# A hybrid encoder block with 32 experts: last expert's results summed by TensorE, row numbers made on GpSimd, logits with operands exchanged, norm stage and first unit in another order

## The reference

```python
u2 = rms_norm(h, norm_ffn_g)
logits = u2 @ router_w + router_b                  # 512 x 32
top_val, top_idx = lax.top_k(logits, 4)
gates = jax.nn.softmax(top_val)
# for each token n, choice k and expert e = top_idx[n, k]:
#   glu, lin = split(u2[n] @ w1[e] + b1[e])        # 1024 -> 2 x 1024
#   act = min(glu,7) * sigmoid(1.702*min(glu,7)) * (clip(lin,-7,7) + 1)
#   y[n, k] = act @ w2[e] + b2[e]                  # 1024 -> 1024
h = h + sum_k gates[n, k] * y[n, k]
out = rms_norm(h, final_norm_g)[:, 16:]
```

## Time and profile before

| | us |
|---|---|
| timed runs, median (lowest, highest) | 1636.83 (1635.07, 1637.48) |
| profiled execution, whole | 1649.01 |
| its span, first to last instruction | 1647.2 |
| PE busy | 1585.5 (96%) |
| DVE, POOL, ACT busy | 650.5, 427.5, 392.4 |
| first dense product starts | 22.21 |
| last dense add on DVE starts | 536.18 |
| first expert starts on PE | 565.95 |
| last product of the last expert ends | 1617.60 |

### The profile page before, as it was taken

The page is one execution under the profiler, slowest core; times in us unless marked ns, Lnnn a source line. Parts: engine busy times, 40 slices in busy tenths (PEclk is TensorE's granted clock), DMA queues, the critical chain, the costliest instruction groups (busy, mean ns, idle before and its releaser), DMA issues.

```text
span 1647.2 us, 38590 instructions
## 1 busy us (share of the span) xinstructions
PE 1585.5 (96%) x16312; PEld 1113.2 (68%) x16312; DVE 650.5 (39%) x1233; ACT 392.4 (24%) x599; POOL 427.5 (26%) x465
## 2 busy tenths in 40 slices
PE   6999999998999889999999999999999999999992
PEld 6998988876889756655556566666666666556551
DVE  3799897025151523322332232224222322232238
ACT  4333134255122512211221111111112111221121
POOL 6334334371433611111111112111211121112114
PEclk9999999999999899999999999999999999999996
DMA  7563243320275289999999999999999999999995
GB/s 212 176 193 118 78 143 89 101 81 22 93 291 195 83 330 412 412 397 410 407 405 392 407 405 399 397 406 406 392 401 408 404 393 407 409 405 392 406 394 208
DMA packets 135055, 497.35 MB, mean 302 GB/s; under 512 B 17417, under 2 KB 76977, under 8 KB 85252
## 3 DMA queue, kind: packets, MB, share of 16 engines
q1 hardware_dynamic: 114452, 467.08, 72.2%
q0 software_dynamic: 8880, 16.54, 3.2%
q10 hardware_dynamic: 11680, 13.12, 2.4%
HBM read 478.41 MB, written 27.36 MB: 307 GB/s over the span
## 4 chain that ended last, share of the span: by engine, by line
PE 91%; ACT 2%; DVE 2%; POOL 2%; DMA 1%; issue 1%; SPq 0%; POOLq 0%; ACTq 0%; DVEq 0%
PE banks L1413 40%; PE banks L1019 25%; PE banks L1462 21%; PE banks L1399 2%; DVE mix_lo L1744 1%; DMA stage<-in_w_in_dram 1%; PE banks L1363 1%; ACT w_hi L733 0%; DMA y_last<-y_rows 0%; ACT banks L924 0%; POOL small L574 0%; PE banks L1433 0%; ACT conv L887 0%; DVE gates L1742 0%; POOL w_lo L596 0%
## 5 line engine op out<-in xcount | busy, mean ns | idle before, releaser
L1413 PE MATMUL banks<-w_ring,xT 128*32 128x512 f32 x6144 | 687.9, 592 | 0.7 <-issue 0.7
L1413 PEld LDWEIGHTS banks<-w_ring,xT 128*32 128x32 f32 x6144 | 359.4, 110 | 287.9 <-issue 122.0
L1462 PE MATMUL banks<-w_ring,actT 128*32 128x256 f32 x6144 | 370.7, 381 | 4.8 <-issue 4.8
L1462 PEld LDWEIGHTS banks<-w_ring,actT 128*32 128x32 f32 x6144 | 249.3, 110 | 110.3 <-issue 18.6
L1843 DVE TENSOR_TENSOR hid<-banks,bias 128x512 f32<-128x512 f32 x96 | 63.9, 666 | 477.2 <-PE banks L1413 475.7
L596 POOL TENSOR_TENSOR w_lo<-stage,w_hi 128x2048 fp32r<-128x2048 f32 x38 | 175.2, 4610 | 268.0 <-ACT w_hi L733 268.0
L1019 PE MATMUL banks<-u_hi,w_hi 128*128 128x264 f32 (+1 forms) x544 | 181.3, 333 | 4.5 <-POOL w_lo L587 4.2
L1019 PE MATMUL banks<-u_hi,w_lo 128*128 128x264 f32 (+1 forms) x544 | 179.9, 331 | 0.0
L1019 PE MATMUL banks<-u_lo,w_hi 128*128 128x264 f32 (+1 forms) x544 | 179.6, 330 | 0.0
L990 ACT ACTIVATE bias<-banks 128x512 f32<-128x512 f32 x32 | 19.1, 597 | 572.5 <-PE banks L1433 572.5
L667 POOL COPY token_now<-token_of 96x1 int32 (+1 forms) x33 | 6.5, 198 | 565.1 <-PE banks L1399 560.6
(11 more groups left out here) (269 smaller groups left out, 1626.4 us busy)
## 6 DMA issues: line engine op xcount, KB each, us to landing
w_ring<-in_expert_w_dram SPq DMA_DIRECT2D x384, 1024.0 KB, 11.5
stage<-in_w_in_dram SPq DMA_DIRECT2D x20, 1024.0 KB, 5.3
y_rows<-empty_row ACTq DMA_DIRECT2D x8, 1280.0 KB, 5.4
stage<-in_w_in_dram SPq DMA_DIRECT2D x16, 512.0 KB, 5.2
y_in<-y_rows SPq DMA_DIRECT2D x4, 2048.0 KB, 12.8
stage<-in_conv_pw_w_dram SPq DMA_DIRECT2D x4, 1024.0 KB, 5.4
stage<-in_mlstm_out_w_dram SPq DMA_DIRECT2D x4, 1024.0 KB, 5.2
stage<-in_w_out_dram SPq DMA_DIRECT2D x4, 1024.0 KB, 5.2
```

The costliest lines, as they stand in the source:

```text
L1413: last = nc.tensor.matmul(banks[32 * g:32 * (g + 1), t].rearrange("p (c j) -> p c j", j=64), xT[:, k, 32 * t:32 * (t + 1)], units, start=k ...
L1462: last = nc.tensor.matmul(banks[32 * g:32 * (g + 1), 3 + t, 0:GRP], actT[:, t, k], w2_ring[k // 2][:, k % 2, GRP * g:GRP * (g + 1)], start ...
```

## The change

Five edits, in one kernel.

**First unit.** PE runs it as three passes of 16 products: hi·hi, then lo tokens, then lo weights, each pass with its own wait. The transposes' banks are renumbered (`PART_BANK`), ACT copies five parts instead of four ahead of the first weights, and DVE makes the meta tokens' low part ahead of the last scaling.

**Norm stage.** DVE norms tile i-1 behind the add of tile i; ACT squares all four tiles before it copies `u2T`; POOL scales three tiles before it makes constants, and only those that the router needs before the fourth.

**Logits.** The router's columns become the stationary operand and 128 tokens the moving one, two rounds of four column groups. ACT copies the four partial sums (`part`), and one product with four stacked unit matrices (`stack4`) adds and turns them back.

**Row numbers.** The multiplication of `row_of` moves to POOL, which alone waits for the twelve loads. The shifts and additions go.

**End.** The last expert is taken out of the loop on PE and POOL, and its results aren't stored. Before it, DVE makes `selT`, gate values at (slot, token), and five diagonal matrices of gates. Behind it, PE multiplies `selT` with `y_out`, a row group of 32 slots and a bank for each column group, and adds five of the sixteen gated blocks by diagonal products. DVE sums the other eleven and adds the banks (`add_products`). Tiles 3 and 2 are scaled by ACT and multiplied by POOL, tiles 1 and 0 by DVE as before. The rows for emptying in DRAM are a fifth fewer.

```diff
+TILE_ORDER = (3, 2, 1, 0)
+SUMS = ((3, 0), (3, 1), (3, 2), (3, 3), (2, 0), (2, 1), (2, 2), (2, 3), (1, 0), (1, 1), (0, 0))
+DIAGONALS = ((1, 2), (1, 3), (0, 1), (0, 2), (0, 3))
+SCALED_BY_POOL = (3, 2)
...
-            sp.wait_ge(y_stored, passes * (16 * TG * NE))
-            last_rows = y_dram[Y_ROWS:Y_ROWS + SEQ * CG].rearrange("(i p r) n -> i p (r n)", i=TT, p=P)
-            for i in range(TT):
-                sp.dma_start(y_last[:, i], last_rows[i]).then_inc(y_loaded[TT], 16)
-            for i in range(TT):
-
-                sp.wait_ge(out_made, i + 1)
+            for m, i in enumerate(TILE_ORDER):
+
+                if i in SCALED_BY_POOL:
+                    sp.wait_ge(out_made_pool, m + 1)
+                else:
+                    sp.wait_ge(out_made, m + 1 - len(SCALED_BY_POOL))
                 sp.dma_start(out[0, P * i:P * (i + 1), :], h_res[:, i]).then_inc(stored, 16)
...
-            ffn_norm(0)
-            ffn_norm(1)
+            for i in range(TT - 1):
+                ffn_norm(i)
 
             pool.wait_ge(mm_done, pair_tick(WO_PAIR + 1, 8))
             nc.gpsimd.memset(no_code, NONE).then_inc(moe_consts, 1)
             nc.gpsimd.iota(code, [[TOPK * P, TT], [1, TOPK]], base=0, channel_multiplier=TOPK)
             nc.gpsimd.iota(expert_id, [[1, NE]], base=0, channel_multiplier=0, allow_small_or_imprecise_dtypes=True)
+            nc.gpsimd.memset(all_ones, 1.0)
+            nc.gpsimd.memset(zeros, 0.0)
+            nc.gpsimd.iota(slot_no, [[1, SLOTS]], base=0, channel_multiplier=0, allow_small_or_imprecise_dtypes=True)
+            chain(nc.gpsimd.memset(earlier, 1.0))
+
+            nc.gpsimd.affine_select(out=earlier, in_=earlier, compare_op=ALU.is_gt, fill=0.0, base=0,
+                                    pattern=[[1, P]], channel_multiplier=-1).then_inc(moe_consts, 1)
+            ffn_norm(TT - 1)
...
-            pool.wait_ge(tables_made, 2)
+            pool.wait_ge(rows_in, 16 * CG * TG)
+            chain(nc.gpsimd.tensor_scalar(row_of, row_of, float(CG), group_of, ALU.mult, ALU.add))
...
+            before = CHUNKS + TT
+            for m, i in enumerate(TILE_ORDER[:2]):
+                pool.wait_ge(squared, before + m + 1)
                 rstd(P, f_square[:, i:i + 1], f_rstd[:, i:i + 1], D, rstd_made)
+            for m, i in enumerate(SCALED_BY_POOL):
+                pool.wait_ge(squared, before + 2 + m + 1)
+                if m == 0:
+                    pool.wait_ge(row_bc_in, 48)
+                nc.gpsimd.tensor_tensor(h_res[:, i], h_res[:, i], last_g, ALU.mult).then_inc(out_made_pool, 1)
+            for m, i in enumerate(TILE_ORDER[2:]):
+                pool.wait_ge(squared, before + 4 + m + 1)
+                rstd(P, f_square[:, i:i + 1], f_rstd[:, i:i + 1], D, rstd_made)
...
-                if j == 4:
+                if j == EARLY:
                     split_hi(0, 0)
...
-                if i:
-                    u2T_part(act, i - 1)
-            u2T_part(act, TT - 1)
+
+            def logit_part(i):
+
+                act.wait_ge(logits_mm, 2 * i + 1)
+                nc.scalar.activation(part[:, i % 2], banks[:, 6 + i % 2, 0:P], ACT.Copy).then_inc(u2T_made, 1)
+
+            u2T_part(act, 0)
+            for i in range(TT):
+                if i + 1 < TT:
+                    u2T_part(act, i + 1)
+                logit_part(i)
 
 
             act.wait_ge(bias_in, 16 * 2 * PARTS)
...
+            for m in range(2):
+                last_square(m)
+            for m, i in enumerate(SCALED_BY_POOL):
+                act.wait_ge(rstd_made, CHUNKS + TT + m + 1)
+                nc.scalar.activation(h_res[:, i], h_res[:, i], ACT.Copy, scale=f_rstd[:, i:i + 1]).then_inc(squared, 1)
+            for m in range(2, TT):
+                last_square(m)
...
 
-            pe.wait_ge(u_lo_made, 2 * TT + 1)
+            def first_terms(n):
+
+                for c in range(2):
+                    for k in range(KT):
+                        hi, lo = weights(0, k, c)
+                        last = nc.tensor.matmul(banks[:, c, 0:HALF], lo if n == 2 else hi, (u_lo if n == 1 else u_hi)[:, k, halves[0]],
+                                                start=n == 0 and k == 0, stop=n == 2 and k == KT - 1)
+                if n == 2:
+                    last.then_inc(mm_done, 1)
+
+            def first_unit():
+
+                pe.wait_ge(u_lo_made, 3)
+                pe.wait_ge(u_hi_made, EARLY)
+                pe.wait_ge(w_hi_made[0], 1)
+                first_terms(0)
+                pe.wait_ge(u_lo_made, EARLY)
+                first_terms(1)
+                wait_weights(0, 0)
+                first_terms(2)
...
+
+                    pe.wait_ge(mask_made, i - 1)
+                for r in range(KT // CG):
+                    for g in range(CG):
+                        k = CG * r + g
+                        last = nc.tensor.matmul(banks[32 * g:32 * (g + 1), 6 + i % 2, 0:P], w_router[:, k], u2T[:, i % 2, k],
+                                                start=r == 0, stop=r == KT // CG - 1, tile_position=(0, 32 * g))
+                last.then_inc(logits_mm, 1)
+
             row_transposes(0)
+            pe.wait_ge(wo_out, TT + 2)
+            row_transposes(1)
             for i in range(TT):
-                if i + 1 < TT:
-                    row_transposes(i + 1)
-                pe.wait_ge(u2T_made, 2 * (i + 1))
-                if i >= 2:
-
-                    pe.wait_ge(mask_made, i - 1)
-                for k in range(KT):
-                    last = nc.tensor.matmul(banks[:, 6 + i % 2, 0:NE], u2T[:, i % 2, k], w_router[:, k], start=k == 0, stop=k == KT - 1)
-                last.then_inc(logits_mm, 1)
+                logit_parts(i)
+                if i + 2 < TT:
+                    row_transposes(i + 2)
+                pe.wait_ge(u2T_made, part_copied(i))
+                nc.tensor.matmul(banks[:, 6 + i % 2, P:P + NE], part[:, i % 2], stack4, start=True, stop=True).then_inc(logits_mm, 1)
...
+                pe.wait_ge(last_set, q + 2)
+                pe.wait_ge(y_made, n * TG + (TG + 1))
+                pe.wait_ge(xT_made, n * 2 + 4)
+                for m, i in enumerate(TILE_ORDER):
+                    first_bank = 0 if m % 2 else 4
+                    mine = [d for d in DIAGONALS if d[0] == i]
+                    if m >= 2:
+                        pe.wait_ge(summed, q * TT + (TT + m - 1))
+                    for t in range(TG):
+                        for g in range(CG):
+                            last = nc.tensor.matmul(banks[:, first_bank + g, 0:GRP], selT[32 * g:32 * (g + 1), t, i], y_out[32 * g:32 * (g + 1), t],
+                                                    start=t == 0, stop=t == TG - 1 and not mine, tile_position=(32 * g, 0))
+                    if mine:
+                        pe.wait_ge(y_loaded[i], q * 16 + 16)
+                    for d in mine:
+                        for g in range(CG):
+                            last = nc.tensor.matmul(banks[:, first_bank + g, 0:GRP], diag[:, DIAGONALS.index(d)],
+                                                    y_in[i][:, d[1], GRP * g:GRP * (g + 1)], start=False, stop=d == mine[-1])
+                    last.then_inc(last_mm, 1)
...
-
-
-            dve.wait_ge(g_in, 32)
-            for i in range(TT):
-                dve.wait_ge(rstd_made, CHUNKS + i + 1)
-                nc.vector.scalar_tensor_tensor(out=u2[:, i], in0=h_res[:, i], scalar=h_rstd[:, i:i + 1], in1=gf_bc,
-                                               op0=ALU.mult, op1=ALU.mult).then_inc(u2_made, 1)
+                    if j and i:
+                        normed_rows(i - 1)
+            normed_rows(TT - 1)
...
+                    for t in range(TG):
+                        own(nc.vector.tensor_tensor(sel_in[:, t], slot_row[:, 32 * t:32 * (t + 1)].unsqueeze(1).to_broadcast(shape),
+                                                    last_rep[:, 0].unsqueeze(2).to_broadcast(shape), ALU.is_equal))
+                    for t in range(TG):
+                        own(nc.vector.tensor_tensor(sel_in[:, t], sel_in[:, t], last_rep[:, 1].unsqueeze(2).to_broadcast(shape), ALU.mult))
+                    nc.vector.tensor_scalar(slot_row, slot_row, float(SLOTS), None, ALU.add)
+                    for d, (i, k) in enumerate(DIAGONALS):
+                        nc.vector.tensor_scalar(diag[:, d], ident, gate_now[:, i, k:k + 1], None, ALU.mult)
+                    nc.vector.transpose(selT.rearrange("p t i c -> p (t i c)"), sel_in.rearrange("p t c s -> p (t c s)")).then_inc(last_set, 1)
...
+                def add_products(m):
+
+                    i, first_bank = TILE_ORDER[m], 0 if m % 2 else 4
+                    dve.wait_ge(last_mm, q * LAST_MMS + (2 + m))
+                    dve.wait_ge(sum_step, q * STEPS_OF_SUM + (3 + SEL_STEPS + max(c for c, (j, _) in enumerate(SUMS) if j == i)))
+                    rows = h_res[:, i].rearrange("p (g n) -> p g n", g=CG)
```

(1 more changed line is left out.)

214 lines of the change are left out of this document (141 added, 73 removed).

## The result

| | before | changed |
|---|---|---|
| timed runs, median (lowest to highest) | 1637.15 (1635.07 to 1637.69) | 1626.72 (1622.37 to 1627.39) |
| profiled execution, span | 1647.2 | 1620.6 |

The ratio is 0.9924, with a 95% interval of 0.9909 to 0.9939. That is a gain of 10.4 us by the medians, and of 12.4 by the ratio, where 23.0 were forecast; 1626.7 lies above the 1614 of the forecast and above its range of 1611 to 1624. The profiles overstate the gain (26.6 us of span), for a reason that turned out to be the centre of the case. All medians and ratios in this document are of fast runs; two of the twelve runs of `half_before_again`, further on, took 3313 and 9277 us and are left out.

What follows compares the result with a forecast made beforehand. PE was taken to bound the kernel through 32 equal expert steps. Gains of 6.0 + 13.0 + 4.0 = 23.0 us, subtracted from the timed median of 1636.83, gave 1613.8, or 1614, with a range of 1611 to 1624.

Steps and rivals of the forecast that it cites:

- the experts are 32 equal steps set by PE: Expert loop: PE alone sets each step of 32.66 us; no piece of the chain is a transfer.
- nothing later would eat the first unit's gain: Behind the first unit: 448 us of chains hang on PE's own progress, so the 6.0 us carries through.
- What bounds the kernel: Whole kernel: PE bounds the experts, with the weight stream near at 402 GB/s; gains lie before, around and after them.
- Edit 1: First unit: regrouped passes remove PE's pause and end it at 24.0 instead of 30.06; 6.0 us gained.
- Edits 2 and 3: Norm, logits and row numbers: expert 1 begins at 593.1 instead of 606.1; 13.0 us gained, bounds 10 and 14.5.
- Edit 4: Kernel end, last expert's results added on PE: 4.0 us gained; bounds 5.5 gained to 8.4 lost.
- rival A: Kernel end: products on different row groups don't overlap, 8.4 us lost there, 1626 in all; chance 0.10.
- the drag that was named: Kernel end: POOL's scale steps held by DVE adds, 1.16 us against 0.19; could cost 3 of the 4 us.
- The sum: Whole kernel: 6.0 + 13.0 + 4.0 = 23.0 us, subtracted unchanged from the timed median of 1636.83.
- The 12.2 us between profile and timed runs: Kernel before: profiled execution 1649.01 against timed median 1636.83; the prediction couldn't place the difference.
- Rival B: Expert 1: the early start is lost waiting 5 us for weights, since refills move less than PE; 1619, chance 0.09.
- Rival C: Expert loop: the stream bounds every expert; at 385 GB/s a step is 34.0, 43 us lost, 1657; chance 0.04.

Runs made afterwards that it cites:

- half_before_again: Kernel before, loading only half the columns of each weight piece from expert 1 on (wrong weights, same instructions); 1636.89 us, ratio 0.9991.
- changed, A: The changed kernel in the first comparison, beside the kernel before at 1637.15 us; 1626.72 us, ratio 0.9924.
- changed, D: The changed kernel run once more, beside the kernel before at 1648.50 us; 1628.68 us, ratio 0.9895.
- before_e1: Kernel before with only the first unit's passes regrouped; 1637.92 us, ratio 0.9988.
- rows_on_dve_third: Changed kernel with the row-number multiplication back on DVE, which waits for the twelve row loads; 1623.35 us, ratio 0.9912 (as rows_on_dve 1634.79 us, 0.9916).
- vecs_first: Changed kernel with SyncE's twelve small loads moved between the two halves of the first weights; 1620.54 us, ratio 0.9888.
- long-step set: Runs whose profiles show 32.5 to 32.7 us an expert; the kernel before took 1648.5 us there.
- short-step: Runs whose profiles show 32.24 us an expert; the kernel before took 1637 to 1638.6 us there.
- before_e12: Kernel before with the first unit's passes, norm stage and logits changed; 1642.86 us, ratio 0.9968, and again 1632.71 us, ratio 0.9967.
- C and E: Two sets of runs, each beside the kernel before, which took 1648.45 us in the first and 1638.43 us in the second.
- set D: Set of runs beside the kernel before at 1648.50 us; the changed kernel took 1628.68 us there, ratio 0.9895.
- early3: Changed kernel with expert 1's first three weight pieces refilled ahead of the wait for the scatters and the table loads; 1618.39 us, ratio 0.9872.

## Why the prediction was wrong

| landmark, profiled | before | changed, A | changed, D | `before_e1` | `rows_on_dve_third` |
|---|---|---|---|---|---|
| last dense add | 536.18 | 534.00 | 532.25 | 534.41 | 532.73 |
| expert 0 starts | 565.95 | 558.26 | 557.95 | 568.36 | 557.29 |
| first second product | 592.20 | 579.21 | 578.90 | 592.22 | 582.99 |
| from it to the last one's end | 1025.40 | 1015.98 | 1022.86 | 1011.87 | 1013.99 |
| from there to the end | 29.6 | 25.4 | 25.1 | 33.4 | 25.0 |

The main step that failed is "the experts are 32 equal steps set by PE", carried from the profile of before to the timed runs. There the weight stream is a bound as well, and it took about 7.7 of the 23.0 us. The second is that nothing later would eat the first unit's gain; a wait and half a clock behind it took 3.8 of its 6.0.

**What bounds the kernel** was right for the profiled execution and wrong for the timed ones. At 32.64 us a step the stream wins back lead, at 32.24 it loses some, as the landing times above show. (13.1 MB at the 408 GB/s of the changed kernel are 32.1 us, but 408 was read at PE's own pace, so it doesn't decide it.) The 13 us that PE moved ahead at expert 1 were the lead the stream had lived on. The median landing of 11 us in the earlier trace rows hid a fall from 13.7 to 10.2, so the sign was in the trace of before: 3.5 us won back over the run is little, and the 0.4 us by which a step must have been shorter in the timed runs is more than the 0.15 a step that was won back.

**Edit 1** (6.0 forecast). The unit itself was right: no pause, done at 24.5. "Nothing later eats this" is the second step that failed. A load landing at 26.16 lay 4 us under the old end of the unit, and no chain of before could show it, since PE came later. With the half clock behind it 2.2 were left, and `before_e1` measures 2.0. (From the old end of the unit to the last dense add it is 506 us, where the prediction speaks of 448; nothing hangs on it.) `vecs_first` brings 3.7 at the last dense add.

**Edits 2 and 3** (13.0). Right between the profiles, 13.4: DVE no longer waits for the row loads, there is no hole and no slow pass. Expert 0 came at 24.3 us (24 forecast), expert 1 at 56.5 (57). The scatters moved 6.8 us instead of 3.8, and PE's first-row products ran at the faster rate. The timed runs of single edits show less of it: 5.4 for edits 1 and 2 together, and 4.6 in a long-step set or nothing in a short-step one for the multiplication on POOL; a part of the 8.6 to 9.0 of the next edit, whose runs hold the six shifts, belongs here.

**Edit 4** (4.0). It was undersized: 4.2 between the first two profiles, 4.8 and 5.8 between those of `before_e12` and `rows_on_dve` in C and E, and 8.6 to 9.0 in their timed runs together with the six shifts. Selection products took 1.4 us a tile (2.0 taken), so rival A is out. POOL's first two scale steps took 1.10 and 1.62 beside DVE's sums, the drag that was named, off the path. The old end varies: it is 33.4 in `before_e1`, where DVE waited 3.03 us for the last results; why they came late isn't shown.

**The sum.** "Since the holes named are waits between engines and not recording, I subtract the same 23.0" is where the first failure entered the number, and it cost most. The 12.2 us between profile and timed runs were the other sign that a step was shorter in the timed runs, and 12.2/31 = 0.39 would have given it: 32.25 us a step.

**Rival B** was the mechanism, at a chance of 0.09 and a price of 5 us. It was put aside by a median landing of 11 us and a least of 6.6, which say how far a stream keeps up with a step of 32.64. Its price was 7.7 us by the ratios, not paid once at expert 1: of 4.6 us of waits in the profiled execution 1.2 fall in the second step, most of the rest after the 23rd. So 23.0 less 3.8 (edit 1) less 7.7 gives 11.5, between the 10.4 of the medians and the 12.4 of the ratio. Rival C had the right cause with a bandwidth of 385 GB/s, which wasn't seen. In set D the bare sum holds, 23.0 - 3.8 = 19.2 against 17.3 to 19.8, but partly by luck: an end worth more than forecast stands in it for row numbers that were worth less.

Shown by experiment: that the stream takes a part of the gain, some 7.7 us (half the bytes, the refills earlier, and no wait for a piece in set D), that the small loads caused the wait and the half clock at the start, the part of the row numbers, and the two lengths of a step. Not shown: what the wait at the start costs at the end of the run in a short-step set, what makes the steps of a set long or short, why landing times rise behind 1400 us in the short-step sets, and the timed runs' 4 us above the profiled one, which I take for more of the same waits.

## What to carry to other kernels

When two resources are as near to each other as here (a step of 32.64 lets the stream recover, one of 32.24 does not), treat them as one bound. Before you sum gains on one, look whether the other wins or loses lead from step to step. Landing times by stretch of the run tell it; their median over the whole run doesn't. When a profiled execution and the timed runs of the same kernel differ by more than the runs scatter, divide the difference by the steps of the loop first; the profile may show another balance than the one that is timed. And behind a wait that is removed look for the transfers that land under it: their landing times are in the trace even where nobody waits for them.

## What the runs showed of the hardware

TensorE goes through the same weight loads in two ways that stay the same for a whole set of runs: 82 us of 200 with loads in flight in `before_e1`, 137 in the changed kernel of set D, at the same granted clock (1.00) and the same 110 ns each, and 32.24 against 32.58 us an expert. What it is, stays open.

A pause of PE doesn't always cost its clock: 4.56 us in `rows_on_dve_third` left it at half for the pass behind it (granted 0.50, 6.23 us), 2.31 in `early3` for most of it (0.50, then 0.65; 5.35 us), and 2.73 in `before_e1` did not (1.00, 3.66 us).

A POOL scatter of 0.96 us takes 3.77 beside a DVE subtraction of 3.35 us of 96x3072 elements in SBUF; one of 3.38 is in the earlier trace rows.

What the DMA engines move falls a little over the run in the changed kernel: 411 GB/s in 700 to 1000 us, 407 in 1000 to 1300, 404 in 1300 to 1560. In the profile of before, where PE sets the pace, it is 402, 401 and 403.
